# RWKV-7 projections: the block behind them merged in, key norm and exponentials under the value projection

## The chip, the cores and the metric

One core of one Trainium2 chip runs the whole program. The metric is the device time of one execution in microseconds; the median of several runs counts. One further execution was taken by the hardware profiler, and all rows below come from that one.

## What is computed

The model step runs four layers over 288 tokens (256 of a prompt, 32 of a running stream), each a mixer followed by an MLP. Layer 2 has the RWKV-7 mixer, and the change lies in its projections:

```python
lerp = lambda j: hf + xx * mix[j]
r = lerp(0) @ w_r
wl = w0 + jnp.tanh(lerp(1) @ w1) @ w2
decay = jnp.exp(-jnp.exp(-jax.nn.softplus(-wl) - 0.5))
k = lerp(2) @ w_k
v = lerp(3) @ w_v
a = jax.nn.sigmoid(a0 + (lerp(4) @ a1) @ a2)
g = jax.nn.sigmoid(lerp(5) @ g1) @ g2
kk = (k * k_k).reshape(B, T, H, N)
kk = kk * lax.rsqrt(jnp.maximum(jnp.sum(kk * kk, axis=-1, keepdims=True), 1e-24))
k = k * (1.0 + (a - 1.0) * k_a)
...
bonus = (jnp.sum(r * k * r_k, axis=-1, keepdims=True) * v).reshape(B, T, D)
```

The per-token recurrence that follows is done in chunks of 32 tokens. For it the projections are scaled by running products of the decay: its logarithm is summed along each chunk (a scan), and exponentials of the sum and of its negative scale r, the keys and the keys' gated form.

## The kernel before

Activations lie with the features on 128 partitions, as 8 tiles of 288 tokens (2304 float32 on each partition). A weight matrix of 1024 by 1024 comes in four chunks of 1 MB. Each chunk is split for accuracy: ScalarE writes a high part (`make_hi`, line 288), VectorE the rest (`make_lo`, line 302), and TensorE runs three products of each tile (`use_chunk`, lines 317 to 319), 48 matmuls a chunk. Four raw buffers and two split buffers rotate; the split of chunk n waits until TensorE has used chunk n-2.

`stage_rwkv` (from line 1509) holds four blocks of code. A block gives each engine an instruction list of its own, written by hand, and no engine goes on to the next block until all have ended theirs.

- The first block (line 1554) has the three projections p = 0 (r), 1 (k), 2 (v): chunks a0 to a0+11. Each fills PSUM banks 0 to 3 (group g = 0), then 4 to 7 (g = 1), which ScalarE copies out (`evict`, line 1641). Between k and v TensorE runs the second low-rank products (line 1624), and ScalarE turns them into the log-decay `logw` and the `rate` by sigmoids (line 1678). During v VectorE scales `logw` by a constant (line 1766), scans it (1768), forms the key factor `temp` (1777, 1783) and the bonus parts (1785); ScalarE forms the scaled keys `t1` and their squares `t2` (1686, 1689). TensorE sums the squares by head at the very end (1630).
- The second block (line 1801) loads two constants, then VectorE clamps and inverts the key norms (1862, 1863), ScalarE takes the root and three exponentials (1811 to 1814), TensorE spreads the norms over each head, sums the bonus parts and forms the gate (`four`, line 1823), VectorE scales t1 and forms the operands of the recurrence (1867 to 1888), and GpSimd scales the keys twice (1851, 1854).
- The third block (line 1943) turns the operands to tokens on partitions by TensorE transposes (line 1960). The fourth is the recurrence and the output projection.

Several tiles share an area of the on-chip memory; which, and until when, decides how early a result may be written.

Of the kernel before, what the change touches and what calls it, by code (L numbers as in the profile page):

```python
# [24 lines left out]
P = 128  # L25
D = 1024
C = D // P
# [120 lines left out]
def build(nc, A, O, const_order):  # L148
# [48 lines left out]
    def const_dram(name, rows=P):  # L197
# [20 lines left out]
        "inner_done", "inner_out", "lora_done", "lora_out", "proj_out")}  # L218
# [1290 lines left out]
    def stage_rwkv():  # L1509
# [14 lines left out]
        t1, t2 = at("t1", unit(10), ARC), at("t2", unit(11), ARC)  # L1524
        ar = at("ar", unit(12), [P, 2, C, T])
        temp = at("rwkv_temp", unit(2), ARC)
# [14 lines left out]
        g2 = at("gate_w2", hi_at, [P, D])  # L1541
# [9 lines left out]
                                                                         "lora_out", "proj_out"))  # L1551
        lora_lerps = (at("lerp_a", unit(2), ARC), at("lerp_g", unit(3), ARC), at("lerp_w", unit(9), ARC))
        splits = ((x_hi, x_lo), (y_hi, y_lo), (x_hi, x_lo))
        with nc.Block() as block:
            @block.sync
            def _(sp):
# [15 lines left out]
                load_ahead(sp, a0 + 5, a0 + 12)  # L1572
                sp.wait_ge(S["store"].sem, S["store"].at(32))

            @block.gpsimd
            def _(pool):
                nc.gpsimd.memset(hs[:, :, 0:1], 0.0).then_inc(pool_s.sem, 1)

            @block.tensor
            def _(pe):  # L1580
# [8 lines left out]
                for p in range(3):  # L1589
                    hi, lo = splits[p]  # L1590
                    for g in range(2):
                        if p == 1:
                            pe.wait_ge(*((inner_out.sem, inner_out.at(4)), (proj_out.sem, proj_out.at(2)))[g])
                        if p == 2:
                            pe.wait_ge(lora_out.sem, lora_out.at(3 + g))
                        for half in range(2):
                            n = a0 + 4 * p + 2 * g + half
                            pe.wait_ge(lo_made, n + 1)
                            if g == 0:
                                pe.wait_ge(in_lo.sem, in_lo.at(2 * p + half + 1))  # L1600
                            use_chunk(n % 2, lambda k: hi[:, half * KT + k, :], lambda k: lo[:, half * KT + k, :],
                                      4 * g, half == 0, half == 1).then_inc(chunk_used, 1)
                    if p == 0:
# [11 lines left out]
                    if p == 1:  # L1615
                        pe.wait_ge(S["load2"].sem, S["load2"].at(64))
                        for s in range(4):
                            j, b = s // 2, 4 * (s % 2)

                            pe.wait_ge(*((proj_out.sem, proj_out.at(3 + s)) if s < 2 else  # L1620
                                         (lora_out.sem, lora_out.at(s - 1))))
                            for m in range(4):
                                c = 4 * (s % 2) + m
# [3 lines left out]
                pe.wait_ge(act_s.sem, act_s.at(1))  # L1627
                pe.wait_ge(proj_out.sem, proj_out.at(5))
                for c in range(C):
                    nc.tensor.matmul(PS[0:HN, 0, 0:T], to_head[:, c, :], t2[:, c, :], start=c == 0, stop=c == C - 1)  # L1630

            @block.scalar
            def _(act):
# [40 lines left out]
                for s in range(4):  # L1674
                    act.wait_ge(lora_s.sem, lora_s.at(s + 1))
                    j, b, c0 = s // 2, 4 * (s % 2), 4 * (s % 2)
                    for m in range(4):
                        ins = nc.scalar.activation((logw, rate)[j][:, c0 + m, :], PS[:, b + m, 0:T], ACT.Sigmoid,
                                                   bias=vec(("rwkv_w0", "rwkv_a0")[j], 0, c0 + m))
# [3 lines left out]
                act.wait_ge(proj_out.sem, proj_out.at(4))  # L1683
                act.wait_ge(in_lo.sem, in_lo.at(6))
                for c in range(C):
                    nc.scalar.activation(t2[:, c, :], k[:, c, :], ACT.Square, scale=vec("rwkv_k_k", 0, c))
                make_hi(act, a0 + 11)
                for c in range(C):
                    ins = nc.scalar.activation(t1[:, c, :], k[:, c, :], ACT.Copy, scale=vec("rwkv_k_k", 0, c))
                ins.then_inc(act_s.sem, 1)  # L1690
                evict(2, 0)
                evict(2, 1)

            @block.vector
            def _(dve):
# [65 lines left out]
                for n in range(a0 + 7, a0 + 10):  # L1761
                    make_lo(dve, n)

                dve.wait_ge(lora_out.sem, lora_out.at(2))
                dve.wait_ge(lerp_s.sem, lerp_s.at(6 * C))
                dve_own.step(dve, V.tensor_scalar(logw[:, :, :], logw[:, :, :], -float(np.exp(-0.5)), None, ALU.mult))
                for c in range(C):
                    V.tensor_tensor_scan(ar[:, 1, c, :], scan_keep[:, :], logw[:, c, :], 0.0, ALU.mult, ALU.add) \
                        .then_inc(dve_own.sem, 1)
                dve_own.n += C  # L1770
                dve.wait_ge(dve_own.sem, dve_own.n)
                make_lo(dve, a0 + 10)
                V.tensor_tensor(logw[:, :, :], ar[:, 1, :, :], logw[:, :, :], ALU.subtract)

                dve.wait_ge(lora_out.sem, lora_out.at(4))
                for c in range(C):
                    V.tensor_scalar(temp[:, c, :], rate[:, c, :], 1.0, vec("rwkv_k_a", 0, c), ALU.subtract, ALU.mult) \
                        .then_inc(dve_own.sem, 1)
                dve_own.n += C
                make_lo(dve, a0 + 11)  # L1780
                dve.wait_ge(dve_own.sem, dve_own.n)
                dve.wait_ge(act_s.sem, act_s.at(1))
                dve_own.step(dve, V.scalar_tensor_tensor(k[:, :, :], temp[:, :, :], 1.0, k[:, :, :], ALU.add, ALU.mult))
                for c in range(C):
                    V.scalar_tensor_tensor(temp[:, c, :], r[:, c, :], vec("rwkv_r_k", 0, c), k[:, c, :],
                                           ALU.mult, ALU.mult)
# [792 lines left out]
```

## Time and profile before

| what | us |
|---|---|
| median of three runs (1452.0 to 1455.12) | 1455.05 |
| the profiled execution, whole time | 1449.8 |
| its span, first to last instruction | 1447.7 |
| first of the four blocks' value projection and block 2 | about 735.7 to 801.9 of the span |

TensorE's matmuls are busy for 90% of the span, VectorE for 58%, ScalarE for 35%, GpSimd for 4%. A row of a timeline reads: start, length of the merged group, engine, line, operation, what is written from what, shape, count, and in brackets how long the engine sat idle before it and what ended that. "PEq" as the releaser means the program went from one block to the next.

### The profile page before, as it was taken

To read this page: it belongs to the slowest core of one execution; us is meant where nothing else is said; L and a number is where in the kernel's file an instruction comes from. 1 tells how busy PE (TensorE), PEld (TensorE's weight loads), DVE (VectorE), ACT (ScalarE), POOL (GpSimd) and SP (SyncE) were. 2 spreads that over 40 slices of the span, in tenths; PEclk is the share of its full clock that TensorE was granted. 3 is DMA by queue.
4 is the path that set the end of the run, shared out by engine and by line. 5 is a ranking of instruction groups with operands and counts; after the bars stand their busy time and mean duration, and the time that the engine had idled before them with its cause. 6 is when DMAs were issued, how large, how long until landed. Compare 5 with 4: busy or idle time off the path is not lost. (4 is left out here: it accounts for less than half of the span.)

```text
span 1447.7 us, 25014 instructions
## 1 busy us (share of the span) xinstructions
PE 1296.1 (90%) x11138; PEld 1234.4 (85%) x11138; DVE 834.1 (58%) x891; ACT 508.6 (35%) x536; POOL 53.8 (4%) x43
## 2 busy tenths in 40 slices
PE   4799999999789999977997587899999975999998
PEld 2699999977689999977885586799999965999998
DVE  4766633667636664349566684666763337667333
ACT  2443332532335333232453322343343223333322
POOL 0100000100001000000002200000000001000000
PEclk9899999998799999998998687899999988999998
DMA  5254454613015445452421000045454431454530
GB/s 188 65 172 154 166 175 154 187 62 98 30 59 174 151 169 174 151 178 80 137 97 37 7 9 6 9 153 166 156 173 168 155 117 54 153 162 158 174 117 33
DMA packets 98912, 174.67 MB, mean 121 GB/s; under 512 B 11700, under 2 KB 19020, under 8 KB 98822
## 3 DMA queue, kind: packets, MB, share of 16 engines
q1 hardware_dynamic: 98500, 173.22, 36.4%
q8 instruction: 75, 1.23, 0.3%
q10 hardware_dynamic: 322, 0.10, 0.0%
q14 instruction: 15, 0.12, 0.0%
HBM read 170.98 MB, written 2.33 MB: 120 GB/s over the span
## 5 line engine op out<-in xcount | busy, mean ns | idle before, releaser
L302 DVE TENSOR_TENSOR w_lo<-raw,w_hi 128x2048 fp32r<-128x2048 f32 (+1 forms) x104 | 237.9, 2288 | 314.7 <-ACT w_hi L288 314.4
L317 PE MATMUL PS<-mlp_x_hi,w_hi 128*128 128x288 f32 x1024 | 306.3, 299 | 12.3 <-DVE mlp_x_lo L390 7.1
L288 ACT ACTIVATE w_hi<-raw 128x2048 fp32r<-128x2048 f32 (+1 forms) x104 | 197.6, 1900 | 334.0 <-PE PS L319 332.1
L318 PE MATMUL PS<-mlp_x_hi,w_lo 128*128 128x288 f32 x1024 | 303.5, 296 | 0.0
L317 PE MATMUL PS<-ff_hi,w_hi 128*128 128x288 f32 x1024 | 303.1, 296 | 0.0
L319 PE MATMUL PS<-mlp_x_lo,w_hi 128*128 128x288 f32 x1024 | 302.5, 295 | 0.0
L318 PE MATMUL PS<-ff_hi,w_lo 128*128 128x288 f32 x1024 | 302.1, 295 | 0.0
L319 PE MATMUL PS<-ff_lo,w_hi 128*128 128x288 f32 x1024 | 301.1, 294 | 0.0
L317 PEld LDWEIGHTS PS<-mlp_x_hi,w_hi 128*128 128x128 f32 x1024 | 193.2, 189 | 15.2 <-issue 11.3
L319 PEld LDWEIGHTS PS<-mlp_x_lo,w_hi 128*128 128x128 f32 x1024 | 194.2, 190 | 0.0
L318 PEld LDWEIGHTS PS<-mlp_x_hi,w_lo 128*128 128x128 f32 x1024 | 193.6, 189 | 0.2
L319 PEld LDWEIGHTS PS<-ff_lo,w_hi 128*128 128x128 f32 x1024 | 192.9, 188 | 0.0
L318 PEld LDWEIGHTS PS<-ff_hi,w_lo 128*128 128x128 f32 x1024 | 192.3, 188 | 0.0
L317 PEld LDWEIGHTS PS<-ff_hi,w_hi 128*128 128x128 f32 x1024 | 191.9, 187 | 0.0
L628 DVE TENSOR_TENSOR w_lo<-raw,w_hi 128x2048 fp32r<-128x2048 f32 x52 | 119.2, 2292 | 106.2 <-ACT w_hi L593 106.2
L593 ACT ACTIVATE w_hi<-raw 128x2048 fp32r<-128x2048 f32 x52 | 99.2, 1908 | 117.5 <-PE PS L319 117.5
L317 PE MATMUL PS<-x_hi,w_hi 128*128 128x288 f32 x376 | 116.0, 308 | 22.5 <-DVE x_lo L1732 11.2
L318 PE MATMUL PS<-x_hi,w_lo 128*128 128x288 f32 x376 | 114.1, 304 | 0.0
L319 PE MATMUL PS<-x_lo,w_hi 128*128 128x288 f32 x376 | 113.7, 302 | 0.0
L317 PEld LDWEIGHTS PS<-x_hi,w_hi 128*128 128x128 f32 x376 | 73.8, 196 | 24.5 <-issue 22.8
L318 PEld LDWEIGHTS PS<-x_hi,w_lo 128*128 128x128 f32 x376 | 73.9, 197 | 0.2
L597 ACT ACTIVATE ff_hi<-relu 128x1152 f32 (+1 forms) x32 | 37.4, 1168 | 104.2 <-DVE relu L635 104.2
(440 smaller groups left out, 1478.6 us busy)
## 6 DMA issues: line engine op xcount, KB each, us to landing
raw<-in_w_up SPq DMA_DIRECT2D x64, 1024.0 KB, 5.3
raw<-in_w_down SPq DMA_DIRECT2D x64, 1024.0 KB, 5.0
raw<-in_attn_w_in SPq DMA_DIRECT2D x6, 1024.0 KB, 6.6
raw<-in_attn_w_out SPq DMA_DIRECT2D x4, 1024.0 KB, 5.1
raw<-in_rwkv_w_r SPq DMA_DIRECT2D x4, 1024.0 KB, 5.0
raw<-in_rwkv_w_k SPq DMA_DIRECT2D x4, 1024.0 KB, 6.3
raw<-in_rwkv_w_v SPq DMA_DIRECT2D x4, 1024.0 KB, 5.1
raw<-in_rwkv_w_o SPq DMA_DIRECT2D x4, 1024.0 KB, 5.0
```

Source lines behind the costliest of these rows:

```text
L288: nc.scalar.activation(w_hi[:, n % SPLITS, :, 0:width], raw[:, n % RAWS, :, 0:width], ACT.Copy) \
L302: nc.vector.tensor_tensor(w_lo[:, n % SPLITS, :, 0:width], raw[:, n % RAWS, :, 0:width], w_hi[:, n % SPLITS, :, 0:width].bitcast(F32), ALU ...
L317: nc.tensor.matmul(out, hi, rhs_hi(k), start=first and k == 0, stop=False)
L318: nc.tensor.matmul(out, lo, rhs_hi(k), start=False, stop=False)
L319: mm = nc.tensor.matmul(out, hi, rhs_lo(k), start=False, stop=last and k == KT - 1)
L593: nc.scalar.activation(w_hi[:, j % 2, :, :], raw[:, j, :, :], ACT.Copy).then_inc(hi_made, 1)
L597: nc.scalar.activation(f_hi[:, bass.ds(4 * g, 4), :], relu[:, :, :], ACT.Square) \
L628: nc.vector.tensor_tensor(w_lo[:, j % 2, :, :], raw[:, j, :, :], w_hi[:, j % 2, :, :].bitcast(F32), ALU.subtract).then_inc(lo_made, 1)
```

## The change

The second block goes away and its work is written into the instruction lists of the first. The two constants are loaded behind chunk a0+10, in an area that the projections have freed. On TensorE the head sums of the squared keys stand between the low-rank products, the last of these waits for the inverted norms, the value projection waits for all sigmoids, the spread norms stand behind its first and second chunk (in banks 4 to 7), its second group waits for the scaled keys, and head sums and gates come after its last chunk. The scaled keys and their squares go from ScalarE to VectorE; the constant on the log-decay becomes the `scale` of the exponentials, and the key factor becomes one ScalarE activation a tile. GpSimd's two multiplies stand in the first block; the second waits for the bonus sums, as its output lies where the bonus parts lay.

The diff, cut to its core (signals, tile addresses and the removed block, told above, are left out):

```diff
             @block.sync
-                load_ahead(sp, a0 + 5, a0 + 12)
+                load_ahead(sp, a0 + 5, a0 + 7)
+                sp.wait_ge(chunk_used, a0 + 8)
+                sp.dma_start(from_head[0:HN, :, :].rearrange("p c n -> p (c n)"), const_dram("from_head", HN)) \
+                    .then_inc(load3.sem, 16)
+                sp.dma_start(g2[:, :], A["rwkv_g2"][0]).then_inc(load3.sem, 16)
+                load_ahead(sp, a0 + 7, a0 + 12)
             @block.gpsimd
+                pool.wait_ge(bonus_parts.sem, bonus_parts.at(1))
+                pool.wait_ge(decays.sem, decays.at(2))
+                nc.gpsimd.tensor_tensor(k[:, :, :], k[:, :, :], shrunk[:, :, :], ALU.mult).then_inc(late_keys.sem, 1)
...
+                pool.wait_ge(bonus_sums.sem, bonus_sums.at(2))
+                nc.gpsimd.tensor_tensor(t2[:, :, :].rearrange(seg, s=CH), k[:, :, :].rearrange(seg, s=CH), LAST_DECAY,
+                                        ALU.mult).then_inc(late_keys.sem, 1)
             @block.tensor
                         if p == 2:
-                            pe.wait_ge(lora_out.sem, lora_out.at(3 + g))
+                            pe.wait_ge(*((lora_out.sem, lora_out.at(4)), (key_scaled.sem, key_scaled.at(2)))[g])
...
+                            if p == 2 and g == 0:
+                                if half == 0:
...
+                                    pe.wait_ge(key_root.sem, key_root.at(1))
+                                    pe.wait_ge(lora_out.sem, lora_out.at(3))
+                                else:
+                                    pe.wait_ge(key_scaled.sem, key_scaled.at(1))
+                                for m in range(4):
+                                    mm = nc.tensor.matmul(PS[:, 4 + m, 0:T], from_head[0:HN, 4 * half + m, :], norm_inv,
+                                                          start=True, stop=True)
+                                mm.then_inc(key_spread.sem, 1)
...
+                            pe.wait_ge(*((proj_out.sem, proj_out.at(3)), (proj_out.sem, proj_out.at(4)),
+                                         (lora_out.sem, lora_out.at(2)), (key_inverse.sem, key_inverse.at(1)))[s])
...
+                            if s == 1:
+                                pe.wait_ge(key_squares.sem, key_squares.at(2))
+                                pe.wait_ge(lora_out.sem, lora_out.at(1))
+                                for c in range(C):
+                                    mm = nc.tensor.matmul(PS[0:HN, 0, 0:T], to_head[:, c, :], key_sq[:, c, :], start=c == 0,
+                                                          stop=c == C - 1)
+                                mm.then_inc(key_sums.sem, 1)
             @block.scalar
+                sigmoids(0)
+                sigmoids(1)
                 make_hi(act, a0 + 9)
+                sigmoids(2)
+                sigmoids(3)
+                act.wait_ge(key_inverse.sem, key_inverse.at(1))
+                nc.scalar.activation(norm_inv, norm_inv, ACT.Sqrt).then_inc(key_root.sem, 1)
...
+                for c in range(C):
+                    ins = nc.scalar.activation(modulation[:, c, :], rate[:, c, :], ACT.Identity, bias=one_less[:, c:c + 1],
+                                               scale=vec("rwkv_k_a", 0, c))
                 make_hi(act, a0 + 10)
+                nc.scalar.activation(grown[:, :, :], ar[:, 1, :, :], ACT.Exp, scale=-RATE).then_inc(decays.sem, 1)
+                nc.scalar.activation(shrunk[:, :, :], ar[:, 1, :, :], ACT.Exp, scale=RATE).then_inc(decays.sem, 1)
+                act.wait_ge(earlier.sem, earlier.at(1))
+                nc.scalar.activation(logw[:, :, :], logw[:, :, :], ACT.Exp, scale=-RATE).then_inc(decays.sem, 1)
                 make_hi(act, a0 + 11)
                 evict(2, 0)
                 evict(2, 1)
+                for q in range(2):
+                    act.wait_ge(gate_pe.sem, gate_pe.at(q + 1))
+                    nc.scalar.activation(gate[:, 4 * q:4 * q + 4, :], PS[:, 4 * q:4 * q + 4, 0:T], ACT.Copy)
             @block.vector
+                make_lo(dve, a0 + 7)
+                key_parts(0)
+                make_lo(dve, a0 + 8)
+                key_parts(1)
+                scans(0)
+                dve.wait_ge(key_sums.sem, key_sums.at(1))
+                step(V.tensor_scalar(norm_inv, PS[0:HN, 0, 0:T], 1e-24, None, ALU.max))
+                V.reciprocal(norm_inv, norm_inv).then_inc(key_inverse.sem, 1)
+                scans(1)
+                make_lo(dve, a0 + 9)
+                V.tensor_tensor(logw[:, :, :], ar[:, 1, :, :], logw[:, :, :], ALU.subtract).then_inc(earlier.sem, 1)
+                scale_keys(0)
+                step(V.tensor_tensor(k[:, :, :], k[:, :, :], modulation[:, :, :], ALU.mult))
                 for c in range(C):
+                    ins = V.scalar_tensor_tensor(temp[:, c, :], r[:, c, :], vec("rwkv_r_k", 0, c), k[:, c, :],
+                                                 ALU.mult, ALU.mult)
+                ins.then_inc(bonus_parts.sem, 1)
                 make_lo(dve, a0 + 10)
+                scale_keys(1)
...
+                step(V.scalar_tensor_tensor(ar[:, 0, :, :], t1[:, :, :], -1.0, logw[:, :, :], ALU.mult, ALU.mult))
                 make_lo(dve, a0 + 11)
+                step(V.tensor_tensor(t1[:, :, :], t1[:, :, :], rate[:, :, :], ALU.mult))
+                V.tensor_tensor(ar[:, 1, :, :], r[:, :, :], grown[:, :, :], ALU.mult).then_inc(receptance.sem, 1)
+                step(V.tensor_tensor(bt[:, :, :], t1[:, :, :], shrunk[:, :, :], ALU.mult))
+                step(V.tensor_tensor(t1[:, :, :].rearrange(seg, s=CH), bt[:, :, :].rearrange(seg, s=CH), LAST_DECAY,
+                                     ALU.mult))
+                for q in range(2):
+                    dve.wait_ge(bonus_sums.sem, bonus_sums.at(q + 1))
+                    V.tensor_tensor(bonus[:, c4, :], PS[:, 4 * q:4 * q + 4, 0:T], v[:, c4, :], ALU.mult) \
+                        .then_inc(bonus_made.sem, 1)
```

Here `key_parts(q)` multiplies four tiles of k by the key vector and squares the product, `scans(q)` scans four tiles, and `scale_keys(q)` multiplies half of t1 by the spread norms in banks 4 to 7. The work of each instruction list not shown is as before.

## Rows read from the trace of the kernel before

**Rows 1.** Page, busy time of each engine over the whole span.
```profile
PE 1296.1 (90%) x11138; PEld 1234.4 (85%) x11138; DVE 834.1 (58%) x891; ACT 508.6 (35%) x536; POOL 53.8 (4%) x43
```

**Rows 2.** Stretches: length, busy (count) PE, PEld, DVE, ACT, POOL; clock; DMA.
```profile
789.00:802.50 13.50, 0.10 (x1) 0.14 (x2) 12.78 (x5) 0.65 (x1) 6.39 (x2) 0.61 0.00 1
802.50:806.00 3.50, 3.50 (x18) 3.50 (x19) 0.02 (x1) 1.02 (x1) 1.27 (x2) 0.54 0.20 42
```

**Rows 3.** Timeline of TensorE, from the low-rank products to the transposes.
```profile
727.67 4.14 PE L1624 MATMUL PS<-lora_inner,decay_w 64*128 64x288 f32 x16
...
735.72 0.40 PE L317 MATMUL PS<-x_hi,w_hi 128*128 128x288 f32 x1
...
750.71 0.37 PE L317 MATMUL PS<-x_hi,w_hi 128*128 128x288 f32 x1 [1.94 <-DVE w_lo L302]
...
765.19 4.05 PE L1630 MATMUL PS<-t,to_head 128*16 128x288 f32 x16
...
773.30 6.42 PE L1823 MATMUL PS<-key_norm_inverse,from_head 16*128 16x288 f32 x16 [1.58 <-DMA gate_w<-in_rwkv_g]
...
802.39 3.55 PE L1960 MATMUL PS<-fixed,v 128*128 128x128 f32 x16 [13.91 <-PEq L1801]
...
805.78 1.91 PE L1960 MATMUL PS<-fixed,ar 128*128 128x128 f32 x16
```

**Rows 4.** Timeline of VectorE, value projection and second block.
```profile
739.34 2.29 DVE L302 TENSOR_TENSOR w_lo<-raw,w_hi 128x2048 fp32r<-128x2048 f32 x1 [13.66 <-ACT w_hi L288]
741.55 1.35 DVE L1766 TENSOR_SCALAR log_decay<-log_decay 128x2304 f32<-128x2304 f32 x1
742.94 5.30 DVE L1768 TENSOR_TENSOR_SCAN ar<-scan_keep,log_decay 128x288 f32<-128x288 f32 x8
...
752.96 2.32 DVE L1777 TENSOR_SCALAR rwkv_temp<-rate,vecs 128x288 f32<-128x288 f32 x8
...
759.98 3.52 DVE L1785 SCALAR_TENSOR_TENSOR rwkv_temp<-r,vecs,bk 128x288 f32<-128x288 f32 x8
769.54 0.45 DVE L1862 TENSOR_SCALAR key_norm_inverse<-PS 16x288 f32<-16x288 f32 x1 [6.04 <-PEq L1554]
770.02 1.94 DVE L1863 RECIPROCAL key_norm_inverse<-key_norm_inverse 16x288 f32<-16x288 f32 x1
...
783.89 1.36 DVE L1867 TENSOR_TENSOR bonus<-PS,v 128x1152 f32<-128x1152 f32 x1 [2.78 <-PE PS L1823]
...
790.35 2.56 DVE L1885 TENSOR_TENSOR ar<-r,decay_to_token 128x2304 f32<-128x2304 f32 x1
792.95 6.31 DVE L1887 TENSOR_TENSOR bk<-t,decay_inverse 128x2304 f32<-128x2304 f32 x1
799.29 2.56 DVE L1888 TENSOR_TENSOR t<-bk,last_decay 128x2304 f32<-128x2304 f32 x1
```

**Rows 5.** Timeline of ScalarE, same stretch.
```profile
727.78 1.13 ACT L1641 ACTIVATE bk<-PS 128x1152 f32<-128x1152 f32 x1 [4.42 <-PE PS L319]
729.92 1.68 ACT L1678 ACTIVATE log_decay<-PS,vecs 128x288 f32<-128x288 f32 x4 [1.00 <-PE PS L1624]
...
750.69 3.50 ACT L1689 ACTIVATE t<-bk,vecs 128x288 f32<-128x288 f32 x8
...
772.00 0.44 ACT L1811 ACTIVATE key_norm_inverse<-key_norm_inverse 16x288 f32<-16x288 f32 x1 [1.21 <-DVE key_norm_inverse L1863]
772.46 1.28 ACT L1812 ACT_TABLE_LOAD   x1
773.75 2.12 ACT L1812 ACTIVATE log_decay<-log_decay 128x2304 f32<-128x2304 f32 x1
```

**Rows 6.** Timeline of GpSimd, its two multiplies of the second block.
```profile
779.98 5.06 POOL L1851 TENSOR_TENSOR bk<-bk,decay_inverse 128x2304 f32<-128x2304 f32 x1 [137.41 <-ACT decay_inverse L1814]
790.59 6.25 POOL L1854 TENSOR_TENSOR t<-bk,last_decay 128x2304 f32<-128x2304 f32 x1 [5.56 <-DVE last_decay L1882]
```

**Rows 7.** Stretch of 2 us behind TensorE's pause in the value projection.
```profile
752.00:754.00 2.00, 2.00 (x10) 2.00 (x10) 2.00 (x5) 2.00 (x6) 0.00 (x0) 0.50 0.80 304
```

More of the change, by code:

```diff
@@ L1626, in _ @@
                             mm.then_inc(lora_s.sem, 1)
[L1627 to L1630, printed above, removed]
+                            if s == 1:
[5 more added lines that the diff above has]
+                                mm.then_inc(key_sums.sem, 1)
+                pe.wait_ge(bonus_parts.sem, bonus_parts.at(1))
+                for q in range(2):
+                    pe.wait_ge(proj_out.sem, proj_out.at(5 + q))
+                    for m in range(4):
+                        mm = nc.tensor.matmul(PS[:, 4 * q + m, 0:T], head_ones, temp[:, 4 * q + m, :], start=True, stop=True)
+                    mm.then_inc(bonus_sums.sem, 1)
+                for q in range(2):
+                    pe.wait_ge(bonus_made.sem, bonus_made.at(q + 1))
+                    for m in range(4):
+                        c = 4 * q + m
+                        mm = nc.tensor.matmul(PS[:, c, 0:T], g2[:, c * P:(c + 1) * P], inner[:, 1, :], start=True, stop=True)
+                    mm.then_inc(gate_pe.sem, 1)
             @block.scalar
@@ L1673, in _, with sigmoids @@
                 evict(1, 1)
-                for s in range(4):
+                def sigmoids(s):
                     act.wait_ge(lora_s.sem, lora_s.at(s + 1))
[L1676 to L1679, printed above, removed]
+                    j, b = s // 2, (0, 4, 4, 0)[s]
+                    for c in range(b, b + 4):
+                        ins = nc.scalar.activation((logw, rate)[j][:, c, :], PS[:, c, 0:T], ACT.Sigmoid,
+                                                   bias=vec(("rwkv_w0", "rwkv_a0")[j], 0, c))
@@ new lines, in scans, with scale_keys @@
+                def scans(q):
+                    dve.wait_ge(lora_out.sem, lora_out.at(q + 1))
+                    for c in range(4 * q, 4 * q + 4):
+                        V.tensor_tensor_scan(ar[:, 1, c, :], scan_keep[:, :], logw[:, c, :], 0.0, ALU.mult, ALU.add) \
+                            .then_inc(summed.sem, 1)
+                def scale_keys(q):
+                    c4 = slice(4 * q, 4 * q + 4)
+                    dve.wait_ge(key_spread.sem, key_spread.at(q + 1))
+                    V.tensor_tensor(t1[:, c4, :], t1[:, c4, :], PS[:, 4:8, 0:T], ALU.mult).then_inc(key_scaled.sem, 1)
@@ L1781, in _ @@
[L1781 to L1786, printed above, removed]
+                scale_keys(1)
+                dve.wait_ge(decays.sem, decays.at(1))
@@ L1890, in stage_rwkv @@
-        load.close(32)
-        act_s.close(4)
-        pe_s.close(6)
-        dve_s.close(6)
-        pool_s.close(2)
         GT = 4 * CH
```

174 lines of the change are left out of this document (60 added, 114 removed).

## The prediction

> **What bounds the kernel now.** I looked first at the page's busy shares: TensorE's matmuls fill 90% of the span [rows 1], so most of the kernel is matmul time that this change doesn't touch, and only a stretch in which TensorE stands can give much. Then I read the rows of 2 us round the mixer, to find where TensorE stands: in the last 13.5 us of the second block it has one instruction, while VectorE is busy for 12.8 us of them [rows 2]. The timelines say why. TensorE's last work of block 2 ends near 788.5, and the next starts at 802.39, behind a pause of 13.91 us that ends with the passage between blocks [rows 3]; VectorE's last multiply starts at 799.29 and takes 2.56, so block 2 ends at 801.85 [rows 4]. From the end of the value projection at 765.2 to 801.85 the chain is short TensorE work alternating with VectorE and ScalarE passes: 36.7 us, of which TensorE works about half. Ahead of it, the value projection (735.72 to 765.19) is bound by TensorE with one pause of 1.94 for a weight split [rows 3]. So the question is how much of the 36.7 us disappears, and how much later the value projection ends.
>
> **The change part by part.** I keep the trace's time axis, start where both kernels are alike (low-rank products at 727.67 [rows 3]) and give 0.1 us to each hand-over between engines, my choice. A set of four low-rank, head-sum, spread or gate tiles is 8 passes: 4.14 / 2 = 2.07 us [rows 3]. A value chunk is (750.71 - 1.94 - 735.72) / 2 = 6.5 us at full clock [rows 3].
>
> *What moves ahead of the value projection.* The eviction of k ends at 728.91, the first sigmoids at 731.6 [rows 5]. VectorE then has half the key parts: four scalings at 2.32 / 8 = 0.29 [rows 4] and a square of 1152 elements, half of 2.56 [rows 4], to 731.5. That is beside TensorE's second set, so the head sums (4.05 us for 8 tiles [rows 3]) run from 731.8 to 735.9. The scans of half the tiles (5.30 / 2 [rows 4]) lie under them. Clamp and reciprocal, 0.45 + 1.94 [rows 4], give the inverse at 738.4. TensorE has its third set under that, waits 0.6, has the fourth from 738.5 to 740.6; its sigmoids (1.68 [rows 5]) end at 742.35. The value projection thus starts at 742.45 instead of 735.72: **6.7 us given away**. Queued behind this wait is all of TensorE's remaining list; on VectorE the wait for the head sums holds the second scans and the low split of a0+9, which end at 741.1 and 743.4, well ahead of their use.
>
> *Inside the value projection.* The first chunk ends at 748.95. ScalarE's table load, root and eight key-factor activations (1.28 + 0.44 + 3.50 [rows 5]) are over by 747.6, under it. The first spread set ends at 751.0. From here VectorE carries the path: half of t1 scaled (1.36 [rows 4]), key factor (2.56 [rows 4]), bonus parts (3.52 [rows 4]), the split of a0+10 (2.29 [rows 4]), second half of t1 (1.36), to about 762.1. TensorE has the second chunk and the second spread set to 759.6 and stands for 2.65 us, since its second group needs both that split and the scaled keys. The third chunk then ends at 768.75. ScalarE's table load and three exponentials, 1.28 + 3 x 2.1 [rows 5], lie between 751.0 and 758.5, off the path; the last high split follows at once, before anyone asks for it. So the exponentials do go under the projection at no cost; uncovered they would cost 7.6.
>
> *GpSimd beside VectorE.* GpSimd's first multiply is released by the bonus parts, at 758.5, just as VectorE goes on to the split of a0+10 without a wait. The nearest rows show what a meeting costs: a VectorE multiply of two on-chip operands of the size that takes 2.56 took 6.31 at 792.95, and GpSimd's multiply, started at 790.59, ended at 796.84 [rows 4, 6]: VectorE ended 2.42 us after it, as if it had stood till then. The one that had begun at 790.35, before GpSimd, took its normal 2.56. The VectorE pass at 783.89 with one operand in PSUM took 1.36 while GpSimd worked [rows 4, 6]. I take it that the first to start goes through and the other stands. The Trainium skill, SBUF — State Buffer, section "Who interferes with whom", says so: a VectorE instruction with two SBUF inputs and a GpSimd one that reads SBUF take turns for a whole instruction, whoever starts first. The trace agrees, with 6.31 against 2.56; by the rule the sum is as it stands here, and without it the block would end 2.8 us earlier.
> With the split ahead, GpSimd runs from 760.8 to 765.85 (5.06 [rows 6]). The t1 scaling reads PSUM and goes through; the operand pass behind it stands until 765.85, and with its 2.56 and the split of a0+11 that split is there at 770.65. TensorE, done at 768.75, stands 2.0 us. Bounds: nothing if they don't meet (end 2.8 us earlier), or 5.06 on the split of a0+10 if GpSimd starts first. I take the middle case, since VectorE's next instruction needs no signal and GpSimd's does (0.24 us lay between the two starts in block 2).
>
> *The clock.* After the pause of 1.94 us TensorE's granted clock was 0.50, the lower of its levels, in 752 to 754 [rows 7], and the two chunks from 750.71 to 765.19 took 14.48 instead of 13.05: 1.4 us for one such pause [rows 3]. The new kernel has pauses of 1.9, 2.65 and 2.0. The second falls on a chunk that the late split of a0+11 covers. I charge one drop, 1.4, with none and two as bounds.
>
> *The tail.* Without the drop the last chunk ends at 777.25. Its eviction takes 1.13 [rows 5], the bonus sums run to 781.4, VectorE's four multiplies (2.56 each, from 770.65) to 780.75, both bonus passes to 783.4, the gates to 786.3, their last copy to 787.5. GpSimd's second multiply starts at 781.6 and needs between 3.9 (6.25 less the 2.3 that it may have stood behind the pass of 790.35) and 6.25 [rows 6]: 785.5 to 787.8, in the shadow of the gates or just level with them. With the one drop the block ends at 788.9, against 801.85: **12.9 us gained**.
>
> *Behind it.* The first transposes took 3.55 us at clock 0.54, after the long pause; the next sixteen 1.91 [rows 2, 3]. Now gates run until 2 us before them, so they should start at the higher level: 1.6 more, with nothing as the other bound.
>
> *Costs at nothing.* The two constant loads stand in SP's queue ahead of the load of a0+11; they are issued at 727.6, that load follows within 1 us and its chunk is asked for near 758, so 30 us of matmuls hide it. VectorE's own constant pass over log-decay (1.35) and the eight key-factor passes (2.32) go away [rows 4]; ScalarE loses two sets of eight (3.50 each) and takes one. All that is inside the times above.
>
> The **sum** is 12.9 + 1.6 = 14.5 us. The profiled execution of 1449.8 would become 1435.3. It lies 5.25 under the median of the runs, 1455.05, so I forecast 1440.5 for the median.
>
> **The rivals.**
> *No meeting, no drop:* GpSimd's multiply and VectorE's don't delay each other, and the clock holds. The end is then 784.75, the gain 17.1 + 1.6, the time 1436.4. Against it stands the 6.31 row.
> *GpSimd first:* it takes the port before the split of a0+10 starts. By the rule of the skill's page named above this would be a whole instruction. By rows, the split ends at 767.5, TensorE stands 8 us, GpSimd is then clear of the later operand pass; the gain is 10.4 + 1.6, 1443.1. With two more drops and 6.25 for the second multiply the gain is 6.5 + 1.6, 1447.0. For it: both start within 0.2 us of each other.
> *A cold value projection (slower than before):* the mixed stretch of 16-row spreads and pauses of about 2 us leaves the clock at the lower level all through the four value chunks. Then each takes 13 us instead of 6.5, the two pauses close, the end is 809.65 and the transposes start cold: 7.8 us lost, 1462.9. It decides for slower once about 65% of the chunks' time is cold (14.5 of the 22.3 us between the two ends). For it: the spreads at 773.30 took 0.40 a pass instead of 0.26 and stayed slow to their end [rows 3]. Against: after the old pause the two chunks together lost only 1.4 us, so full matmuls had brought the clock back [rows 3].
> *The change doesn't do what it says:* the waits only change places. If about half of the value chunks is cold, gain and loss cancel and the time stays within 4 us of 1455.
>
> **How the numbers follow.** Forecast 0.62, no meeting 0.12, GpSimd first 0.15, waits that cancel 0.05, cold projection 0.06. The range from 1436.0 to 1449.0 holds the first three with 2 us for the scatter of the runs, and leaves 0.11 out. About 0.3%, 4.4 us, is what a measurement can tell from no change. Faster by more: 0.89; within: 0.05; slower: 0.06.
>
> **What would show it.** Right: the value projection starts near 742.4; TensorE stands about 2.7 us before a0+10, for VectorE, and 2 us before a0+11; an operand pass of VectorE of 5 to 6 us beside GpSimd's first multiply; exponentials over before the last high split; transposes near 789 and warm. Wrong: a split of over 5 us ahead of a0+10, a clock of 0.5 over more than one chunk, a later start than 744, or a GpSimd end that is last by over 2 us.

## Result, and the profile after

The changed kernel takes **1439.7 us**, median of six runs (1436.63 to 1445.26), against 1455.09 for six runs of the kernel before on the same chip. The ratio is 0.9908, 95% interval 0.9883 to 0.9933. That is 15.4 us by the medians and 13.4 by the ratio; 14.5 were forecast. One execution of the kernel before, among those beside the second group of experiments, took 2154.18 us at a clock of 0.554, and neither the ratios nor the median of 1453.42 given there count it.

The page (busy time of each engine) hardly differs from [rows 1]; no gain of this size can be read there:

```profile
PE 1300.5 (90%) x11138; PEld 1242.4 (86%) x11138; DVE 835.0 (58%) x893; ACT 505.9 (35%) x528; POOL 53.6 (4%) x43
```

The two spans would mislead too: 1447.7 before, 1443.5 after. The profiled execution of the changed kernel was the longest of its six. So I cut each trace in three: ahead of the low-rank products, from there to the first transposes (**the stretch**, in which all the moved work lies), and the rest. The stretch goes from 727.67 to 802.39 before [rows 3], 74.72 us, and from 729.88 to 792.41 after, 62.53 us: **12.2 us** shorter. The rest went from 645.3 to 651.1 in these two executions; the first experiment asks why.

TensorE's timeline of the changed kernel (start, duration, line, output from inputs, count; in brackets the pause ahead and what ended it):

```profile
729.88 4.14 PE L1660 MATMUL PS<-lora_inner,decay_w 64*128 64x288 f32 x16
733.95 4.05 PE L1667 MATMUL PS<-key_sq,to_head 128*16 128x288 f32 x16
...
740.52 2.20 PE L1660 MATMUL PS<-lora_inner,rate_w 64*128 64x288 f32 x8 [0.38 <-DVE lora_inner L1864]
744.49 0.61 PE L319 MATMUL PS<-x_hi,w_hi 128*128 128x288 f32 x1 [1.76 <-ACT rate L1729]
...
753.47 2.20 PE L1637 MATMUL PS<-lora_inner,from_head 16*128 16x288 f32 x8
...
767.35 0.61 PE L319 MATMUL PS<-x_hi,w_hi 128*128 128x288 f32 x1 [1.45 <-DVE t L1849]
...
781.66 4.04 PE L1674 MATMUL PS<-rwkv_temp,fixed 128*128 128x288 f32 x16
786.80 4.15 PE L1680 MATMUL PS<-lora_inner,gate_w 128*128 128x288 f32 x16 [1.10 <-DVE bonus L1898]
792.41 1.94 PE L1975 MATMUL PS<-fixed,v 128*128 128x128 f32 x16 [1.46 <-PEq L1567]
```

The head sums now stand between the low-rank sets, the spread sets between the value chunks, and the pause of 13.91 ahead of the transposes [rows 3] is 1.46. The first sixteen transposes take 1.94 instead of 3.55. VectorE's timeline of the same kernel, from the first spread set on:

```profile
755.71 1.35 DVE L1849 TENSOR_TENSOR t<-t,PS 128x1152 f32<-128x1152 f32 x1 [8.04 <-PE PS L1637]
...
759.57 3.52 DVE L1873 SCALAR_TENSOR_TENSOR rwkv_temp<-r,vecs,bk 128x288 f32<-128x288 f32 x8
763.01 2.29 DVE L304 TENSOR_TENSOR w_lo<-raw,w_hi 128x2048 fp32r<-128x2048 f32 x1
765.94 1.35 DVE L1849 TENSOR_TENSOR t<-t,PS 128x1152 f32<-128x1152 f32 x1 [0.65 <-PE PS L1637]
767.22 3.10 DVE L1879 COPY last_decay<-decay_to_token 128x72 f32<-128x72 f32 x1
770.24 2.55 DVE L1884 SCALAR_TENSOR_TENSOR ar<-t,log_decay 128x2304 f32<-128x2304 f32 x1
772.82 2.29 DVE L304 TENSOR_TENSOR w_lo<-raw,w_hi 128x2048 fp32r<-128x2048 f32 x1
...
785.39 2.62 DVE L1898 TENSOR_TENSOR bonus<-PS,v 128x1152 f32<-128x1152 f32 x2
```

From 755.71 to 788.01 VectorE shows idle time once, 0.65 us, and the gates that close the stretch wait for its last passes (1.10, above). So the tail is bound by VectorE's sum of passes now, a wait inside the copy of 3.10 included. GpSimd's two multiplies in the same kernel, which in [rows 6] took 5.06 and 6.25:

```profile
763.18 7.06 POOL L1598 TENSOR_TENSOR bk<-bk,decay_inverse 128x2304 f32<-128x2304 f32 x1 [118.37 <-DVE rwkv_temp L1873]
785.88 4.08 POOL L1602 TENSOR_TENSOR late_keys<-bk,last_decay 128x2304 f32<-128x2304 f32 x1 [15.64 <-PE PS L1674]
```

And five stretches of the same kernel (bounds; length; busy time and count of PE, PEld, DVE, ACT, POOL; granted clock; DMA share; GB/s):

```profile
738.00:742.00 4.00, 3.62 (x15) 2.56 (x15) 3.92 (x5) 1.67 (x4) 0.00 (x0) 1.00 0.16 60
...
744.00:750.00 6.00, 5.51 (x23) 5.51 (x24) 3.67 (x2) 5.97 (x12) 0.00 (x0) 0.51 0.52 175
750.00:756.00 6.00, 6.00 (x38) 5.11 (x37) 0.29 (x1) 2.68 (x3) 0.00 (x0) 1.00 0.01 3
756.00:760.00 4.00, 4.00 (x22) 4.00 (x21) 3.96 (x3) 3.99 (x3) 0.00 (x0) 0.59 0.00 0
766.00:772.00 6.00, 4.65 (x25) 4.65 (x26) 6.00 (x3) 0.80 (x1) 4.24 (x1) 0.72 0.54 175
```

TensorE's clock falls to its lower level three times: behind the pause of 1.76, inside the second chunk, and behind the pause of 1.45. One such drop was charged.

### The profile page after: what moved, and what is told of

It reads as the page before. It is cut to its first block and busy times, and to the rows that moved or that the text cites. A ratio compares the mean times of both kernels' runs of the same rounds, so it can differ in the third digit from the quotient of the medians.

```text
span 1443.5 us, 25002 instructions
## 1 busy us (share of the span) xinstructions
PE 1300.5 (90%) x11138; PEld 1242.4 (86%) x11138; DVE 835.0 (58%) x893; ACT 505.9 (35%) x528; POOL 53.6 (4%) x43
## 5 line engine op out<-in xcount | busy, mean ns | idle before, releaser
L319 PE MATMUL PS<-x_hi,w_hi 128*128 128x288 f32 x376 | 119.2, 317 | 23.8 <-DVE x_lo L1799 11.2
L320 PE MATMUL PS<-x_hi,w_lo 128*128 128x288 f32 x376 | 117.0, 311 | 0.0
L319 PEld LDWEIGHTS PS<-x_hi,w_hi 128*128 128x128 f32 x376 | 76.7, 204 | 26.5 <-issue 21.0
L321 PEld LDWEIGHTS PS<-x_lo,w_hi 128*128 128x128 f32 x376 | 76.6, 204 | 0.0
```

What stands on the lines that cost most here:

```text
L319: nc.tensor.matmul(out, hi, rhs_hi(k), start=first and k == 0, stop=False)
L320: nc.tensor.matmul(out, lo, rhs_hi(k), start=False, stop=False)
L321: mm = nc.tensor.matmul(out, hi, rhs_lo(k), start=False, stop=last and k == KT - 1)
```

## The experiments

The theory, after the two traces: (1) what the change gains lies inside the stretch, 12.2 us and 1.6 behind it; (2) the exponentials under the value projection carry most of it; (3) what is left of the stretch is set by VectorE's passes, held up by GpSimd, and only ahead of that by the lower clock. Rivals: a real loss behind the stretch (645.3 to 651.1), the clock as the bound of all of it, or the two folded passes as the source of the gain. Times of the stretch run from the first low-rank product to the first transpose in each run's trace.

**The same kernel again, and the kernel before again.** No edit.

> The changed kernel unaltered, profiled once more. From the first low-rank product to the first transpose it took 62.5 us in the first trace (729.88 to 792.41), against 74.7 before; from there to the end of the span 651.1 against 645.3 before. Theory: the 5.8 us given back behind the mixer's projections are the clock's phase in one execution, not the change; then this trace has 62.5 within 1.5 us in the first part and another value, nearer to 645, in the second. Rival: the recurrence itself runs slower behind the shorter projections; then the second part is again 650 to 652.

Measured: 1439.07 us beside 1451.69 for the kernel before, ratio 0.9903 (0.9873 to 0.9932); stretch 62.57, rest 644.6. Its first transposes:

```profile
793.03 1.94 PE L1975 MATMUL PS<-fixed,v 128*128 128x128 f32 x16 [1.46 <-PEq L1567]
```

> The kernel before unaltered, profiled once more, to see how far two executions of one kernel differ by stretch. In its first trace 74.7 us lay between the first low-rank product and the first transpose, and 645.3 from there to the end of the span; the changed kernel had 62.5 and 651.1, then 62.5 and 644.6. Theory: the stretch of the projections repeats within 1.5 us, the rest scatters by several us with the clock. Rival: the rest repeats too, near 645.

Measured: 1453.73 beside 1453.42, ratio 0.9999 (0.998 to 1.0019); stretch 74.50, rest 648.6. So the stretch repeats within 0.3 us, and the rest scatters by 3.3 and by 6.5 us between two executions of one kernel (645.3 and 648.6 before, 651.1 and 644.6 after). The loss behind the stretch is within that scatter and did not come again; that rival falls, and from here the stretch is the measure.

**GpSimd's first multiply cut to an eighth.** It now makes one tile of eight and leaves seven out.

```diff
-nc.gpsimd.tensor_tensor(k[:, :, :], k[:, :, :], shrunk[:, :, :], ALU.mult).then_inc(late_keys.sem, 1)
+nc.gpsimd.tensor_tensor(k[:, 0:1, :], k[:, 0:1, :], shrunk[:, 0:1, :], ALU.mult).then_inc(late_keys.sem, 1)
```

> GpSimd's first multiply does one of eight tiles and leaves seven out, so it holds nothing for long. In the changed kernel VectorE's copy of the last decays took 3.1 us beside it where 0.2 was its time before. Theory: the split of a0+11 comes 2.9 us earlier, but chunk a0+10 ends no earlier, so only VectorE's tail shortens; projections 60.9 us instead of 62.5, the whole 1 to 2 us faster than the changed kernel. Rival: the meeting is on the path of every engine, projections 59.6. Second rival: it costs nothing, 62.5.

Measured: stretch 61.37, 1.2 us less; 1439.24, ratio 0.9908 (0.988 to 0.9936), in which 1.2 us can't be seen. GpSimd, then VectorE, in this kernel:

```profile
760.79 2.77 POOL L1598 TENSOR_TENSOR bk<-bk,decay_inverse 128x288 f32<-128x288 f32 x1 [118.44 <-DVE rwkv_temp L1873]
```

```profile
764.84 0.22 DVE L1879 COPY last_decay<-decay_to_token 128x72 f32<-128x72 f32 x1
...
781.83 2.83 DVE L1898 TENSOR_TENSOR bonus<-PS,v 128x1152 f32<-128x1152 f32 x2 [1.73 <-PE PS L1674]
```

The copy of the last decays takes 0.22 where it took 3.10: it was the copy that stood behind GpSimd. The 2.9 us that VectorE wins there shorten the stretch by 1.2 only, because VectorE now waits 1.73 for the bonus sums: TensorE is next in line at once.

**64 rows for the spread sets.** The 16-row passes of the spread are extended by 48 rows in which the constant is zero.

```diff
-sp.dma_start(from_head[0:HN, :, :].rearrange("p c n -> p (c n)"), const_dram("from_head", HN)) \
+sp.dma_start(from_head[0:N, :, :].rearrange("p c n -> p (c n)"), const_dram("from_head", N)) \
...
-mm = nc.tensor.matmul(PS[:, 4 + m, 0:T], from_head[0:HN, 4 * half + m, :], norm_inv,
+mm = nc.tensor.matmul(PS[:, 4 + m, 0:T], from_head[0:N, 4 * half + m, :], inner[0:N, 2, :],
```

> The spread of the norms multiplies 64 rows (48 of them zero weights) instead of 16; pass count and length are unchanged. In the changed kernel TensorE's clock fell to 0.50 at about 757 without a pause ahead of it, just behind the first 16-row spread set. Theory: passes of 16 rows leave the clock low like a pause; then with 64 rows the chunk behind the first spread set takes 6.5 us instead of 8.2 and the projections 60.5 to 61.5 instead of 62.5. Rival: pauses alone set the clock; then the drop stays and the projections take 62.5.

Measured: stretch 62.57, unchanged; 1438.92, ratio 0.9916 (0.9886 to 0.9945). One stretch and three rows of TensorE in this kernel:

```profile
756.00:760.00 4.00, 4.00 (x31) 4.00 (x32) 3.96 (x3) 3.99 (x3) 0.00 (x0) 1.00 0.00 0
```

```profile
762.43 2.20 PE L1637 MATMUL PS<-lora_inner,from_head 64*128 64x288 f32 x8
766.84 0.40 PE L319 MATMUL PS<-x_hi,w_hi 128*128 128x288 f32 x1 [2.21 <-DVE t L1849]
...
775.41 0.40 PE L319 MATMUL PS<-x_hi,w_hi 128*128 128x288 f32 x1 [0.39 <-DVE w_lo L304]
```

The clock between 756 and 760 is 1.00 instead of 0.59, and the second spread set begins 32.3 us after the stretch's start instead of 33.8. But the pause behind it grows from 1.45 to 2.21 and one of 0.39 appears before the last chunk: both wait for VectorE. The 1.5 us are won on TensorE and handed back to VectorE's chain, so the 60.5 to 61.5 that I expected did not come, though the clock did what the expectation said. That 16 rows alone bring the lower clock is not shown: the reordered kernel below has two such sets and keeps 1.00.

**The two folded passes alone, in the kernel before.** Block order of before; the factor of the decay goes into the exponentials' scale, the key factor's affine pass to ScalarE.

```diff
-dve_own.step(dve, V.tensor_scalar(logw[:, :, :], logw[:, :, :], -float(np.exp(-0.5)), None, ALU.mult))
...
-    V.tensor_scalar(temp[:, c, :], rate[:, c, :], 1.0, vec("rwkv_k_a", 0, c), ALU.subtract, ALU.mult) \
...
-nc.scalar.activation(logw[:, :, :], logw[:, :, :], ACT.Exp).then_inc(act_s.sem, 1)
+nc.scalar.activation(logw[:, :, :], logw[:, :, :], ACT.Exp, scale=-RATE).then_inc(act_s.sem, 1)
...
+    ins = nc.scalar.activation(temp[:, c, :], rate[:, c, :], ACT.Identity, bias=one_less[:, c:c + 1],
+                               scale=vec("rwkv_k_a", 0, c))
```

> The kernel before with only the two VectorE passes folded into ScalarE: the constant of the log-decay as a scale of the exponentials, the key factor by eight ScalarE activations. Theory: VectorE loses 1.35 us ahead of the split of a0+10, for which TensorE stood 1.94 us; the pause shrinks to about 0.6 and may no longer drop the clock, so the projections take 71.9 to 73.3 us instead of 74.7 and the kernel is 1.4 to 2.8 us faster than before. Rival: VectorE has slack enough, no change (74.7).

Measured: 1451.96, ratio 1.0001 (0.9984 to 1.0019); stretch 72.51, 2.2 us less than before. TensorE in this kernel:

```profile
750.09 0.37 PE L317 MATMUL PS<-x_hi,w_hi 128*128 128x288 f32 x1 [0.54 <-DVE w_lo L302]
...
763.05 4.05 PE L1632 MATMUL PS<-t,to_head 128*16 128x288 f32 x16
...
771.19 7.10 PE L1830 MATMUL PS<-key_norm_inverse,from_head 16*128 16x288 f32 x16 [1.61 <-DMA gate_w<-in_rwkv_g]
...
804.40 2.86 PE L1967 MATMUL PS<-fixed,ar 128*128 128x128 f32 x16
```

The weight split comes earlier now, the pause of 1.94 [rows 3] is 0.54 and costs no drop (clock 1.00 from 750 to 763), and the value projection ends 2.9 us earlier, 34.6 us after the stretch's start instead of 37.5. Of this the colder spread passes take 0.7 (7.10 against 6.42 [rows 3]), and the second sixteen transposes give 1.0 back (2.86 against 1.91 [rows 3]), still at the lower clock behind a pause of 14.59. What is left, about 1 us, no timing here can tell from nothing, and the 1.4 to 2.8 us that I expected of the whole time did not show, though the interval leaves room for up to 2.3. At 2.2 us in the stretch the folds are not the main source of the 12.2.

**The exponentials late.** In the changed kernel, the three exponentials go behind the last high split and the value projection's first eviction.

```diff
+make_hi(act, a0 + 11)
+evict(2, 0)
...
-make_hi(act, a0 + 11)
-evict(2, 0)
```

> The changed kernel with one part undone: ScalarE's table load and three exponentials stand behind the split of a0+11 and the first eviction of v instead of ahead of them. Theory: the exponentials were free only because they lay under the value projection; now they run from about 767 to 774.5 (axis of the first trace after), VectorE's operand pass and with it the split of a0+11 wait for them until about 779, TensorE stands some 4 us before its last chunk and loses a clock drop; projections 67 to 69 us instead of 62.5, the kernel 4 to 6 us slower than the changed one. Rival: only the moved norm chain counts; 62.5 as before.

Measured: stretch 70.86, **8.3 us longer**; 1447.85, ratio 0.9969 (0.9948 to 0.9989). ScalarE, GpSimd, VectorE and TensorE in this kernel:

```profile
764.62 1.28 ACT L1751 ACT_TABLE_LOAD   x1
...
769.96 2.11 ACT L1754 ACTIVATE log_decay<-log_decay 128x2304 f32<-128x2304 f32 x1
```

```profile
770.20 5.12 POOL L1598 TENSOR_TENSOR bk<-bk,decay_inverse 128x2304 f32<-128x2304 f32 x1 [127.67 <-ACT decay_inverse L1752]
```

```profile
772.18 5.56 DVE L1884 SCALAR_TENSOR_TENSOR ar<-t,log_decay 128x2304 f32<-128x2304 f32 x1 [3.87 <-ACT log_decay L1754]
777.77 2.29 DVE L304 TENSOR_TENSOR w_lo<-raw,w_hi 128x2048 fp32r<-128x2048 f32 x1
```

```profile
780.12 0.61 PE L319 MATMUL PS<-x_hi,w_hi 128*128 128x288 f32 x1 [6.96 <-DVE w_lo L304]
```

My expectation for this run was too small. It left out what the late exponentials drag behind them: VectorE's operand pass waits 3.87 for them, then starts behind GpSimd and takes 5.56 instead of 2.55, the split of the last weights stands in VectorE's order behind it, and TensorE waits 6.96 for the split. The exponentials still lie under the third chunk here (764.62 to 772.07); what the 8.3 us measure is the chain that waits for them, not their own length. So having them early is worth 8.3 of the 12.2 us in this kernel. How the other 3.9 divide between the key norm under the projection and the dropped block was not tried.

**Order that keeps TensorE fed.** In the changed kernel: the value projection's first group writes the other four banks, so that it needs only the third low-rank set; the second spread set stands in the middle of the second chunk; VectorE makes the splits of the last two chunks before the passes nobody waits for, and its last operand pass behind the bonus.

```diff
-pe.wait_ge(*((lora_out.sem, lora_out.at(4)), (key_scaled.sem, key_scaled.at(2)))[g])
+pe.wait_ge(*((lora_out.sem, lora_out.at(3)), (key_scaled.sem, key_scaled.at(2)))[g])
...
-          4 * g, half == 0, half == 1).then_inc(chunk_used, 1)
+          4 * (1 - g if p == 2 else g), half == 0, half == 1,
+          midway=(lambda: spread(1)) if (p, g, half) == (2, 0, 1) else None) \
...
+make_lo(dve, a0 + 10)
+scale_keys(1)
...
+make_lo(dve, a0 + 11)
```

> The changed kernel with its two pauses taken away: the value projection's first group uses banks 4 to 7, so that it waits for the third sigmoids and not the fourth; the second spread set stands in the middle of the second chunk; VectorE makes both splits ahead of the bonus parts and operand passes, and its last operand pass behind the bonus. GpSimd's two multiplies stay. Theory: TensorE goes through the four chunks with at most one pause of 1 us, and the projections take 57 to 59 us instead of 62.5, since GpSimd's first multiply then holds VectorE's first operand pass for 5 us. Rival: VectorE's sum of passes is the bound, whatever their order: 61 to 62.5.

Measured: stretch 63.68, 1.1 us **longer** than after; 1442.16, ratio 0.9939 (0.9921 to 0.9957). One stretch, VectorE's two longest passes, GpSimd, and TensorE's second spread set, bonus sums and gates in this kernel:

```profile
738.00:776.00 38.00, 37.62 (x237) 33.66 (x237) 34.05 (x25) 22.55 (x26) 7.32 (x1) 1.00 0.27 87
```

```profile
764.49 7.53 DVE L1893 SCALAR_TENSOR_TENSOR ar<-t,log_decay 128x2304 f32<-128x2304 f32 x1
...
777.24 6.33 DVE L1898 TENSOR_TENSOR bk<-t,decay_inverse 128x2304 f32<-128x2304 f32 x1
```

```profile
762.28 7.32 POOL L1598 TENSOR_TENSOR bk<-bk,decay_inverse 128x2304 f32<-128x2304 f32 x1 [117.63 <-DVE rwkv_temp L1883]
777.08 4.07 POOL L1602 TENSOR_TENSOR late_keys<-bk,last_decay 128x2304 f32<-128x2304 f32 x1 [7.48 <-PE PS L1679]
```

```profile
754.63 2.20 PE L1635 MATMUL PS<-lora_inner,from_head 16*128 16x288 f32 x8
...
772.86 4.04 PE L1679 MATMUL PS<-rwkv_temp,fixed 128*128 128x288 f32 x16
785.01 6.96 PE L1686 MATMUL PS<-lora_inner,gate_w 128*128 128x288 f32 x16 [8.11 <-DVE bonus L1903]
```

TensorE is busy 37.62 of 38.00 us at clock 1.00, and yet the end comes later. My 57 to 59 was wrong and the rival, VectorE's sum, right in kind, though its 61 to 62.5 was too low as well. VectorE meets GpSimd twice now and loses 5.0 and 3.8 us (7.53 and 6.33 against 2.55). TensorE, early, waits 8.11 us for VectorE's bonus passes and then has its gates at the lower clock, 6.96 instead of 4.15.

**The same order, and GpSimd's first multiply on VectorE**, with the 64-row spread.

```diff
-pool.wait_ge(bonus_parts.sem, bonus_parts.at(1))
-pool.wait_ge(decays.sem, decays.at(2))
-nc.gpsimd.tensor_tensor(k[:, :, :], k[:, :, :], shrunk[:, :, :], ALU.mult).then_inc(late_keys.sem, 1)
...
+V.tensor_tensor(k[:, :, :], k[:, :, :], shrunk[:, :, :], ALU.mult).then_inc(late_keys.sem, 1)
```

> As the kernel labelled reordered, and besides GpSimd's first multiply is done by VectorE (2.56 us) and the spread uses 64 rows. Theory: VectorE no longer stands for 5 us behind GpSimd, and the clock does not fall behind a spread set; projections 54 to 56.5 us, the kernel 6 to 8 us faster than the changed one. Rival: VectorE's added pass takes back what the missing wait gives, 57 to 59 us as in reordered.

Measured: stretch **54.77**, as expected; 1434.17 beside 1453.42, ratio 0.9894 (0.9869 to 0.9918; the medians alone give 0.987). Then this kernel and the changed one in turn on one chip:

> The changed kernel unaltered, beside the two kernels below on one chip. From the first low-rank product to the first transpose it took 62.5 us in both traces so far; the rest of the span took 643 to 651 in ten traces of eight kernels. Both theories: 62.5 again, and a median near 0.99 of before.

> The kernel labelled better, on the chip of the changed kernel. Its projections took 54.8 us in its trace, 7.8 less. Theory: the gain in the stretch arrives in the whole time, so its median lies 5 to 9 us under that of the changed kernel. Rival: later stretches give a part back, and the medians differ by 1 to 4 us.

Measured, beside 1451.96 for the kernel before: the changed kernel 1436.8, ratio 0.9906 (0.9882 to 0.993), stretch 62.56; this kernel **1431.9** (1430.84 to 1433.03), ratio 0.9862 (0.9842 to 0.9881), stretch 54.78. By the medians 4.9 us, just under the 5 to 9 of the theory and over the 1 to 4 of its rival, though the stretch is 7.8 shorter: in the two profiled executions the stretch began 1.8 later and the rest took 0.8 more, the scatter already seen. The two intervals only just miss each other, so that it is faster is better borne out by the stretches than by the times. One stretch, VectorE's passes, and TensorE's bonus sums and gates in this kernel:

```profile
738.00:774.00 36.00, 35.62 (x230) 32.10 (x229) 32.04 (x25) 22.55 (x26) 0.00 (x0) 1.00 0.28 95
```

```profile
763.65 2.55 DVE L1890 SCALAR_TENSOR_TENSOR ar<-t,log_decay 128x2304 f32<-128x2304 f32 x1
...
774.02 2.56 DVE L1896 TENSOR_TENSOR bk<-bk,decay_inverse 128x2304 f32<-128x2304 f32 x1
...
779.15 3.99 DVE L1904 TENSOR_TENSOR t<-bk,last_decay 128x2304 f32<-128x2304 f32 x1
```

```profile
772.03 4.04 PE L1676 MATMUL PS<-rwkv_temp,fixed 128*128 128x288 f32 x16
778.02 4.15 PE L1683 MATMUL PS<-lora_inner,gate_w 128*128 128x288 f32 x16 [1.95 <-DVE bonus L1901]
```

VectorE does one multiply of 2.56 more than in the reordered kernel, yet ends its bonus passes 6.1 us earlier in the stretch (50.3 against 56.5 after its start), because it no longer stands ahead of them. The gates' wait is 1.95 and they run at full clock, 2.8 us less. That is the 8.9 between 63.68 and 54.78.

**That multiply on VectorE alone**, in the order of the changed kernel.

> The changed kernel with one edit alone: GpSimd's first multiply is done by VectorE behind its pass with the negative exponentials. Theory: the wait of 2.9 us behind GpSimd goes and a pass of 2.56 us comes, both on VectorE's list and with the clock drops unaltered, so the projections take 62.2 us, within 0.5 of the changed kernel; the 54.8 of better needs the order and this edit together. Rival: GpSimd's multiply alone holds the stretch, and this edit alone gives 57 to 59 us.

Measured: stretch 62.26; 1438.87, ratio 0.9913 (0.9892 to 0.9933). VectorE in this kernel:

```profile
767.77 0.22 DVE L1876 COPY last_decay<-decay_to_token 128x72 f32<-128x72 f32 x1
...
783.07 2.56 DVE L1891 TENSOR_TENSOR bk<-bk,decay_inverse 128x2304 f32<-128x2304 f32 x1
```

The 2.9 us saved on the copy are spent on the multiply. So neither half does it: the order alone loses 1.1, the multiply alone gains 0.3, both together gain 7.8. The 64-row spread, which the fastest kernel also has, shows no share in that: TensorE's bonus sums begin 43.1 us after the stretch's start with 16 rows in the reordered kernel (772.86) and with 64 rows in the fastest (772.03), both at clock 1.00.

## Why the prediction was right

1439.7 came for 1440.5, well inside 1436 to 1449, and the mechanism was the one forecast. But two of its steps were wrong and cancelled, so that the end lies within 1 us of the forecast by luck. On the axis of the prediction (2.21 us off the times of the changed kernel):

| step | forecast | measured |
|---|---|---|
| value projection starts | 742.45 | 742.28 |
| first spread set starts | 748.95 | 751.26 |
| pause before a0+10 | 2.65 | 1.45 |
| third chunk (a0+10) starts | 762.25 | 765.14 |
| split of a0+11 ready | 770.65 | 772.90 |
| pause before a0+11 | 2.0 | none |
| last chunk ends | 778.65 | 779.45 |
| gates copied, block ends | 788.9 | 789.91 |
| first transposes | 1.9 | 1.94 |

**What moves ahead of the projection: right.** The pauses of 0.38 and 1.76 and the set lengths (4.14, 4.05, 2.20) put the start 0.2 us from the forecast. 6.7 us were given away as worked out.

**Inside the projection: the clock was mis-sized.** The step "I charge one drop, 1.4" failed. There were three, and the first chunk, taken at 6.5 us with none, lasted 8.98 (744.49 to 753.47). The second chunk took 8.1 instead of 6.5: the clock fell with no pause ahead, behind the 16-row spread set (in the reordered kernel two such sets left it at 1.00). The last two took 14.3 instead of 13.0. That is 2.5 + 1.6 + 1.3 = 5.4 us, against 1.4. The first came behind the pause of 1.76 and cost 2.5 us, where the pause of 1.94 before had cost 1.4 [rows 3]; the clock was 1.00 until 742, with the sets ahead of that pause done at full speed, and in the reordered kernel, which has the same sets without that pause, there is no drop. The lower clock also came sooner and stayed longer: the first matmul behind the pause took 0.61 us instead of 0.37 [rows 3], and the clock was 0.50 up to 749.7. Why the shorter pause cost more was not tried.

**Why the end is only 1.0 us late.** The first drop is on the path: the first spread set comes 2.3 us late, VectorE stands 8.04 for it, and everything behind comes as late, the split of a0+11 by 2.25. The other two are not. The second delays the second spread set, for which VectorE waits only 0.65 us before it stands behind GpSimd anyway, and the 64-row run takes that drop away without moving the end. The third fills what would have been a pause: the split was ready at 775.11, within 0.3 us of the third chunk's end. So no pause of 2.0 was seen, and the one drop charged had no place of its own: 2.25 late less 1.4 charged is the 0.8 in the table; the tail adds 0.2.

**GpSimd beside VectorE: right mechanism, wrong instruction.** Who starts first was called rightly: the split at 763.01, GpSimd's multiply at 763.18, which stood until 765.30 and then needed 4.94. But "the operand pass behind it stands" was wrong: the copy of 72 elements ahead of that pass stood, 3.10 for 0.22. The wait is the same and the pass begins when GpSimd ends, 770.24, so the term is right in size and the instruction is not. The prediction's sum leaves the copy out. The Trainium skill, SBUF — State Buffer, section "Who interferes with whom", names copies among the instructions that can, if their operands meet its conditions, enter a mode that takes the port pair shared with GpSimd; the trace agrees, with 3.10 here, 3.85 in the 64-row run and 0.22 where GpSimd's multiply was short or gone.

**The exponentials: right that they are free there, the price not shown.** "Uncovered they would cost 7.6" is their own length. No run uncovers them: the late ones cost 8.3, but they ran under the third chunk, and the 8.3 came from the wait for them, a meeting with GpSimd on the path (5.56 for 2.55), TensorE's 6.96 and the lower clock behind it. That the two numbers are close is luck.

**The tail: right.** By the forecast's own times VectorE's multiplies set the first bonus pass, and that the gates (780.75 + 1.36 + 4.14 = 786.25), with TensorE's bonus sums, over at 781.4, 0.7 us short of being the bound. (770.65 and four times 2.56 make 780.89, not 780.75.) So it came: VectorE reaches the bonus passes at 785.39 without a wait, and the gates wait 1.10 for them. Shortening GpSimd's multiply turned it round (a wait of 1.73 for TensorE), so the two bounds lie within 2 us. The second GpSimd multiply took 4.08, near the lower end of 3.9 to 6.25. ScalarE's key factor took 4.24 instead of 3.50, under the first chunk, at no cost.

**Behind it: right.** 3.55 - 1.94 = 1.6, as summed. Stretch and transposes together give 12.2 + 1.6 = 13.8 for the 14.5.

**The rivals.** A cold value projection fell: the clock was down for parts of three chunks (0.51, 0.59 and 0.72 in the stretches shown), but 1.00 from 750 to 756, and it came back inside each of the three. No meeting fell by the 3.10 and 7.06. "GpSimd first" did not happen in this kernel, though by 0.17 us only; its 767.5 for the split is by its rows the end of the scaling behind the split (758.5 + 5.06 + 2.29 + 1.36 = 767.2). Waits that cancel fell with the 12.2 us: the new pauses are 3.6 us in sum (0.38, 1.76, 1.45), with 5.4 of drops, of which 2.3 are on the path.

## What to carry to other kernels

When a block is bound by a chain of short steps on several engines, look for what in it doesn't depend on the long matmul stretch ahead and put it under that; here having the exponentials early was worth 8.3 of 12.2 us. After that, add up each engine's passes from its first release to the end: the engine without idle time is the bound, and keeping TensorE busy at full clock gains nothing (63.68 against 62.56 us) until that sum is shorter. Giving VectorE a pass back can shorten the sum, when the pass on GpSimd made VectorE stand for longer than the pass takes (2.56 against 5.0).

## What the runs showed of the hardware

In the changed kernel a set of eight passes with 16 rows, 2.20 us without a pause on either side, was followed by the lower clock (0.59 in 756 to 760); the same set with 64 rows was not (1.00). That is no rule for 16 rows: in the reordered kernel two such sets, at 749.11 and 754.63, were followed by 1.00. There no drop had come before; in the changed kernel the clock had been at 0.50 until 749.7. Whether that decides was not tried.

A VectorE pass with two on-chip operands that met a running GpSimd multiply ended 2.4 us after it in all five cases read: 799.26 and 796.84 before [rows 4, 6]; 777.74 and 775.32 with the late exponentials; 772.02 and 769.60, 783.57 and 781.15 in the reordered kernel; 783.14 and 780.73 in the fastest one. These are as if it stood and then did nearly its whole work, 2.55 by itself. Between two VectorE passes in a row a waiting GpSimd multiply seems to get in: in the reordered kernel it started with the split at 762.28, took 7.32 where 5.06 is its time in [rows 6], as if it had stood until the split's end at 764.57, and the next pass then took 7.53, with no idle time shown ahead of it.

A copy of 72 elements is held up like a large pass: 3.10 and 3.85 against 0.22.
